# A decoder layer with expert retrieval: seven gather buffers in place of eight, and normalised rows kept in SBUF

## The chip, the cores and the metric

One core of a Trainium2 chip. The time is that of the device, in microseconds (us), for one execution of the whole layer; several executions give a median. Engines: TensorE (PE; PEld is its weight load), VectorE (DVE), ScalarE (ACT), GpSimd (POOL) and SP, which issues DMAs only.

## The reference, cut to what matters

One layer for a prompt of 1024 tokens and a sample group of 8 x 8 tokens, all in float32:

```python
xn = rms_norm(x, attn_norm); proj = xn @ w_in
mixed = concat(differential_attention(proj), rwkv7_time_mixing(proj))
h = x + mixed @ w_out
hn = rms_norm(h, ffn_norm)                 # the "normalised rows"
# PEER retrieval, for each row of hn:
q = hn @ wq                                # 8 heads x 2 x 128
s = q . sub_keys                           # 128 scores per head and half
eidx, gate = top 16 of the 16 x 16 best pairs, softmax
u, v = u_tab[eidx], v_tab[eidx]            # 1024 floats each
y = sum over 8 heads x 16 experts of gate * gelu(u . hn) * v
out = rms_norm(h + y, final_norm)
```

Each row gathers 128 experts, and each expert is one row of 2048 floats (u beside v), 8 KB.

## The kernel before, in words

The rows are cut into nine tiles: t = 0 to 7 of 128 prompt rows each, and t = 8 (`LAST`) of 64 sample rows. One program on every engine holds five stages as Python generators, and each engine issues its part of every stage in the same interleaved order: `run` (L312) first plays `FILL` (L202), which holds the whole input projection and the stages of tiles 0 and 1 ahead of the gathers, then goes through the gather slots, n = 0 to 1087. A tile has 128 slots (64 for the last), and `slots[n]` is (t, j, h): j numbers groups of eight rows, h the head. After each slot the generators of later tiles are pulled by a plan (`pulls`, L261): during the window of tile t (its 128 slots) the time mixing, attention and output stage of tile t + 2 run, and the top-k choice of tile t + 1.

What a slot does, for 8 rows x 16 experts = 128 experts:

- GpSimd gathers 128 expert rows into `buf[n % NBUF]` (L994), 1.05 MB, one row of 8 KB per partition. It waits until the slot that used the buffer before, n - NBUF, has been summed (`v_used`, L993). `NBUF` is 8 (L134).
- VectorE multiplies the u half with `hnR` and sums it into `dot` (L2262). `hnR` holds the group's eight normalised rows, each repeated on 16 partitions.
- ScalarE takes the gelu (L1684) and makes the gate matrix `Z` (L1690), two slots later (`ACT_LAG`).
- TensorE sums gate times v into `psO` (L1413, `v_sum`), three slots later (`SUM_LAG`).

Once per group of eight slots TensorE builds `hnR` for the next group: `repeat_hn` (L1388) multiplies the selection `pick` (made by ScalarE, L1658) with the tile's normalised rows `hn`, into `psH`, in two halves at slots h = 2 and 5. ScalarE copies them to `hnR` (L1666).

The normalised rows come from the output stage, `project_out`. ScalarE squares `op_h` (L1627, into `op_hn` as a throw-away output, with the sum kept) and takes the root; VectorE scales `op_h` into `op_hn` (L2127); TensorE transposes it for the query scores (L1351). SP stores `op_hn` to `scratch_hn_rows` in HBM (L834). At slot 118 of each window (L891) SP's `load_hn` (L852) waits for that store and for the tile's last repeat, and loads the rows of tile t + 1 into `hn`, one place of [128, 1024]. Tile 0's rows are loaded during the fill (L838). A repeat waits for `hn_in` (L1392).

SP issues all other transfers in its own program order: stores of the projection, loads of weights (`op_w`, two of 2 MB, and `op_wkr`, four of 2 MB, per tile), the rows of `h`, y and so on. At step 25 of the output stage it waits, before loading the next tile's time-mixing rows (`load_p`), for `hn_turned`, for the store of `h` and for that of `op_hn` (L842 to L844).

SBUF is laid out by hand; `ip_*` tensors of the projection lie over `buf`, `hnR`, `hn` and `y`, which the gathers use later. So GpSimd starts the gathers only when all the projection's stores have landed (`ip_stored`, L988).

Of the kernel before, what the change touches and what calls it, by code (L numbers as in the profile page):

```python
# [21 lines left out]
ALU = mybir.AluOpType  # L22
# [3 lines left out]
P = 128  # L26
D = 1024
# [81 lines left out]
def rows(t, n=P):  # L109
    return bass.ds(t * P, n)  # L110
# [20 lines left out]


LAST = NT - 1
NBUF = 8  # L134
NZ = 4
QW = 2 * NK
NJ = P // 8
# [145 lines left out]
def peer(nc, T):  # L283
# [100 lines left out]
    with ExitStack() as ctx:  # L384
# [75 lines left out]
            ip_r = e.sb("r", [P, 3, NT])  # L460
        buf = [m.sb(f"buf{b}", [P, 2 * D]) for b in range(NBUF)]
        hnR = m.sb("hnR", [P, 2, D])
        hn = m.sb("hn", [P, D])
        y = m.sb("y", [P, 4, QUART])

        mix = m.sb("mix", [P, D])
# [158 lines left out]
            hn_stored hn_turned hnT scores_done sc_copied""")  # L625
        wk_in = [m.sem(f"op_wk_in{i}") for i in range(2)]
        block = ctx.enter_context(nc.Block())

        def quarters(ap, t):

# [12 lines left out]
        def _(sp):  # L643
# [164 lines left out]
            def project_out(t):  # L808
                R = rows_of(t)

                def load_wk(c_):
                    if t == 0 and c_ == 0:
                        fold_stored()
                    sp.dma_start(wkr[:, c_ % 2].rearrange("p c k n -> p c (k n)"), wk_rows[c_]
                                 ).then_inc(wk_in[c_ % 2], 16)

                for k in range(OP_STEPS):
                    if k == 0:
                        sp.wait_ge(at["o_ready"], t + 1)
                        if t == LAST:  # L820
                            load_w_out(0)
                            load_w_out(1)
                        sp.dma_start(op_h[0:R], T["x"][rows(t, R), :]).then_inc(op["h_in"], 16)
                        sp.dma_start(op_gf[:], T["ffn_norm"].partition_broadcast(P)).then_inc(op["gf_in"], 16)
                    if k == 14:
                        sp.wait_ge(op["summed"], 2 * t + 2)
                        load_wk(0)
                        load_wk(1)
                    if k == 15:
                        sp.wait_ge(op["added"], t + 1)  # L830
                        sp.dma_start(T["h"][rows(t, R), :], op_h[0:R]).then_inc(op["h_stored"], 16)
                    if k == 17:
                        sp.wait_ge(op["hn_ready"], t + 1)
                        sp.dma_start(hn_rows[rows(t, R), :], op_hn[0:R]).then_inc(op["hn_stored"], 16)  # L834
                    if k in (21, 24):
                        sp.wait_ge(op["scores_done"], NC * t + (k - 18) // 3)
                        load_wk((k - 21) // 3 + 2)
                    if k == 25 and t == 1:  # L838
                        sp.wait_ge(ip["summed"], NT)
                        load_hn(0)  # L840
                    if k == 25 and t < LAST:
                        sp.wait_ge(op["hn_turned"], 2 * t + 2)  # L842
                        sp.wait_ge(op["h_stored"], 16 * (t + 1))
                        sp.wait_ge(op["hn_stored"], 16 * (t + 1))  # L844
                        load_p(t + 1)
                    yield

# [2 lines left out]
                    yield  # L850

            def load_hn(t):  # L852
                R = rows_of(t)
                sp.wait_ge(op["hn_stored"], 16 * (t + 1))
                if t:
                    sp.wait_ge(f["hnR_done"], 2 * NJ * t)
                sp.dma_start(hn[0:R, :], hn_rows[rows(t, R), :]).then_inc(f["hn_in"], 16)

            def load_gy(t):

# [18 lines left out]
            def slot(n):  # L879
                t, k = n // PER, n % PER  # L880
                if n == 0:
                    project_stored(NU)
                    load_y(0)
                if t and k == 4:
                    load_gy(t)
                if t and k == 20:
                    store_y(t - 1)
                if t and k == 32:
                    sp.wait_ge(f["y_stored"], 64 * t)
                    load_y(t)  # L890
                if t < LAST and k == 118:  # L891
                    load_hn(t + 1)

            run(slot, {"ip": project, "tm": mix_in_time, "at": attend, "op": project_out, "topk": topk})
            store_y(LAST)
# [104 lines left out]
        def _(pe):  # L1000
# [326 lines left out]
            def project_out(t):  # L1327
                R = rows_of(t)
                for k in range(OP_STEPS):
# [18 lines left out]
                    if k == 17:  # L1348
                        pe.wait_ge(op["hn_ready"], t + 1)
                        for n in range(KD):  # L1350
                            last = nc.tensor.transpose(B[:, n // 4, n % 4 * P:n % 4 * P + R], op_hn[0:R, n * P:(n + 1) * P],  # L1351
                                                       ident[0:R, 0:R])
                            if n % 4 == 3:
                                last.then_inc(op["hn_turned"], 1)
# [33 lines left out]
            def repeat_hn(g_, half):  # L1388

                t, j, _ = slots[g_ * PH]  # L1390
                if half == 0:
                    pe.wait_ge(f["hn_in"], 16 * (t + 1))  # L1392
                    pe.wait_ge(f["pick_ready"], g_ + 1)
                pe.wait_ge(f["hnR_ready"], 2 * g_ + half)
                nc.tensor.matmul(psH[:], pick[:].rearrange("p i k -> p (i k)"),  # L1395
                                 hn[:, half * 512:(half + 1) * 512], start=True, stop=True).then_inc(f["hnR_done"], 1)

            def sum_y(t):

# [36 lines left out]
        def _(act):  # L1436
# [179 lines left out]
            def project_out(t):  # L1616
                R = rows_of(t)
                for k in range(OP_STEPS):
# [5 lines left out]
                                                 ACT.Copy).then_inc(op["copied"], 1)  # L1624
                    if k == 15:
                        act.wait_ge(op["added"], t + 1)
                        nc.scalar.activation(op_hn[0:R], op_h[0:R], ACT.Square, accum_out=st[0:R, 16:17]  # L1627
                                             ).then_inc(op["squared"], 1)
                        act.wait_ge(op["squared"], t + 1)
                        nc.scalar.activation(st[0:R, 17:18], st[0:R, 16:17], ACT.Sqrt, bias=eps[0:R, 0:1],  # L1630
                                             scale=1.0 / D).then_inc(op["root"], 1)
# [61 lines left out]
            def slot(n):  # L1693
                t, j, h = slots[n]
                if n == 0:
                    act.wait_ge(const_in, 16 * CONSTS_IN)
                    make_pick(0)
                    repeat_hn(0, 0)
                    repeat_hn(0, 1)
                if n - h + PH < TOTAL:  # L1700
                    if h == 0:
                        make_pick(n // PH + 1)
                    if h in (4, 7):
                        repeat_hn(n // PH + 1, (h - 4) // 3)
                if n >= ACT_LAG:
                    gate(n - ACT_LAG)
                if t and n == begin(t) + 5:
                    norm_y(t - 1)
                if t and n == begin(t) + 11:
                    root_y(t - 1)  # L1710
# [9 lines left out]
        def _(dve):  # L1720
# [394 lines left out]
            def project_out(t):  # L2115
                R = rows_of(t)
                for k in range(OP_STEPS):
# [5 lines left out]
                    if k == 16:  # L2123
                        dve.wait_ge(op["root"], t + 1)
                        dve.wait_ge(op["gf_in"], 16 * (t + 1))
                        chain(nc.vector.reciprocal(st[0:R, 18:19], st[0:R, 17:18]))
                        nc.vector.scalar_tensor_tensor(op_hn[0:R], op_h[0:R], st[0:R, 18:19], op_gf[0:R], ALU.mult,  # L2127
                                                       ALU.mult).then_inc(op["hn_ready"], 1)
                    yield

# [251 lines left out]
```

## Time and profile before

| | us |
|---|---|
| median of 3 runs | 3982.27 |
| lowest, highest | 3975.95, 3983.49 |
| the profiled execution | 3977.58 |
| its span in the profile | 3975.8 |

The profile is of one execution. Its page gives for each engine the busy time (part 1), the course over 40 equal slices (part 2, with the clock granted to TensorE and the rate of the DMA engines), the DMA queues (part 3), the chain of work that ended last, followed back from the end (part 4), and the costliest groups of instructions with the idle time before them and what ended it (part 5). Beside the page the trace was asked for the timeline of single engines, for windows and for single lines. Gathers run from 747.7 us to 3944.7 us.

### The profile page before, as it was taken

The numbers are of one execution on the slowest core, as the hardware profiler recorded it, in microseconds if no ns is written. First come the engines' busy times: TensorE is split into PE (matmuls) and PEld (weight loads), VectorE is DVE, ScalarE is ACT, GpSimd is POOL, SyncE is SP. The second block draws the span as 40 slices with busy tenths as digits, with TensorE's granted clock in tenths as the row PEclk, the third lists the DMA queues.
The fourth block names the chain that finished last, engine by engine and source line by source line (L and its number), as shares of the span: only waits on it lengthen the run. The fifth ranks groups of instructions, "written<-read, shape, count | busy, mean of one in ns | idle before, by whom it ended". The sixth has DMA issues, their size and how long they took to land.

```text
span 3975.8 us, 54677 instructions
## 1 busy us (share of the span) xinstructions
PE 2853.9 (72%) x20366; PEld 1358.9 (34%) x20366; DVE 2600.8 (65%) x5836; ACT 1284.4 (32%) x3597; POOL 1358.7 (34%) x1190
## 2 busy tenths in 40 slices
PE   6899999675667576766766766677566758867564
PEld 3654454342224232322332243224222415521111
DVE  2423455488668848884987598658866776445954
ACT  1311211324333424342434334433433234422222
POOL 1000000243344434443434343434333456534443
PEclk9999999877877787788778777788787666777655
DMA  9535414899999999999999999999999999999998
GB/s 311 196 141 182 175 67 165 330 400 397 420 416 394 409 421 407 416 402 419 411 404 387 417 409 409 388 417 406 387 409 392 352 375 411 381 399 420 407 405 350
DMA packets 254682, 1431.66 MB, mean 360 GB/s; under 512 B 27376, under 2 KB 45312, under 8 KB 110160
## 3 DMA queue, kind: packets, MB, share of 16 engines
q0 software_dynamic: 163232, 1162.26, 72.1%
q1 hardware_dynamic: 91184, 265.89, 17.7%
q8 instruction: 161, 2.64, 0.3%
q14 instruction: 105, 0.86, 0.1%
HBM read 1373.21 MB, written 54.85 MB: 359 GB/s over the span
## 4 chain that ended last, share of the span: by engine, by line
PE 38%; DMA 32%; DVE 21%; issue 4%; ACT 2%; POOL 2%; SPq 0%; DVEq 0%; ACTq 0%; POOLq 0%
DMA pe_buf<-in_experts,pe_idx 28%; PE ip_B L1027 9%; DVE pe_buf L2262 7%; PE pe_psO L1413 5%; PE pe_B L1361 4%; PE pe_psH L1395 3%; PE pe_B L1344 3%; DMA op_wkr<-scratch_wk_rows 2%; PE pe_B L1061 1%; PE pe_B L1212 1%; DMA ip_w<-in_w_in 1%; POOL pe_buf L994 1%; DVE pe_top L2032 1%; DMA op_w<-in_w_out 1%; PE pe_B L1253 1%
## 5 line engine op out<-in xcount | busy, mean ns | idle before, releaser
L994 POOL DMA_INDIRECT pe_buf<-in_experts,pe_idx x1088 | 1277.3, 1174 | 2500.6 <-PE pe_psO L1413 1702.5
L2262 DVE CUSTOM_DVE_ANT_0 pe_buf<-pe_buf,pe_hnR 128x1024 f32<-128x1024 f32 x1088 | 1319.2, 1224 | 781.6 <-DMA pe_buf<-in_experts,pe_idx 768.5
L1413 PE MATMUL pe_psO<-pe_buf,pe_Z 128*32 128x256 f32 x8704 | 830.1, 485 | 547.2 <-ACT pe_Z L1690 510.4
L1413 PEld LDWEIGHTS pe_psO<-pe_buf,pe_Z 128*32 128x32 f32 x8704 | 222.9, 124 | 1187.3 <-ACT pe_Z L1690 888.3
L1684 ACT ACTIVATE pe_gelu<-pe_dot 128x1 f32<-128x1 f32 x1088 | 217.3, 200 | 1273.1 <-DVE pe_dot L2262 1270.3
L1395 PE MATMUL pe_psH<-pe_hn,pe_pick 128*128 128x512 f32 x544 | 402.9, 831 | 63.9 <-ACT pe_hnR L1666 61.6
L1027 PE MATMUL ip_B<-ip_w,ip_xT 128*128 128x512 f32 (+1 forms) x1008 | 433.3, 580 | 16.6 <-DMA ip_w<-in_w_in 16.6
L1690 ACT ACTIVATE pe_Z<-pe_gl,pe_gelu 128x8 f32<-128x8 f32 x1088 | 327.2, 301 | 43.0 <-ACT pe_gelu L1684 0.4
L1361 PE MATMUL pe_B<-op_wkr,pe_mix 128*128 128x512 f32 (+1 forms) x576 | 264.9, 604 | 9.2 <-DMA op_wkr<-scratch_wk_rows 9.2
L1027 PEld LDWEIGHTS ip_B<-ip_w,ip_xT 128*128 128x128 f32 x1008 | 190.8, 195 | 213.5 <-issue 208.1
L1666 ACT ACTIVATE pe_hnR<-pe_psH 128x512 f32<-128x512 f32 x272 | 159.0, 584 | 49.5 <-PE pe_psH L1395 48.8
L1395 PEld LDWEIGHTS pe_psH<-pe_hn,pe_pick 128*128 128x128 f32 x544 | 107.5, 243 | 193.7 <-ACT pe_hnR L1666 95.9
L1344 PE MATMUL pe_B<-op_w,op_mT 128*128 128x512 f32 (+1 forms) x288 | 153.2, 661 | 11.9 <-DMA op_w<-in_w_out 11.9
L1361 PEld LDWEIGHTS pe_B<-op_wkr,pe_mix 128*128 128x128 f32 (+1 forms) x576 | 101.8, 185 | 144.4 <-issue 143.9
L1781 DVE TENSOR_TENSOR ip_o<-ip_o,ip_mu 128x512 f32<-128x512 f32 (+1 forms) x36 | 22.5, 625 | 163.4 <-ACT ip_o L1454 159.2
L1246 PE MATMUL pe_B<-pe_ident,at_prob 128*128 128x128 f32 x144 | 37.3, 419 | 115.5 <-DVE at_prob L2040 115.5
L1212 PE MATMUL pe_B<-tm_Tn,tm_ML 64*64 64x64 f32 x1312 | 61.8, 256 | 73.8 <-DVE tm_Tt L1912 51.0
L1684 ACT ACT_TABLE_LOAD x79 | 101.4, 1283 | 1.4
L2262 DVE DVE_READ_ACCUMULATOR2_ANT pe_dot<- 128x1 f32 x1088 | 89.3, 82 | 0.0
L1454 ACT ACTIVATE ip_o<-ip_B,ip_r 128x512 f32<-128x512 f32 (+1 forms) x45 | 29.0, 644 | 186.4 <-PE ip_B L1027 183.5
L1212 PEld LDWEIGHTS pe_B<-tm_Tn,tm_ML 64*64 64x64 f32 x1312 | 55.2, 167 | 98.1 <-DVE tm_Tt L1912 59.7
L1142 PE MATMUL pe_B<-tm_Tt,tm_X 64*64 64x64 f32 x1312 | 87.4, 240 | 0.0
(344 smaller groups left out, 3616.5 us busy)
## 6 DMA issues: line engine op xcount, KB each, us to landing
op_wkr<-scratch_wk_rows SPq DMA_DIRECT2D x36, 2048.0 KB, 11.8
ip_w<-in_w_in SPq DMA_DIRECT2D x18, 2048.0 KB, 9.1
op_w<-in_w_out SPq DMA_DIRECT2D x18, 2048.0 KB, 19.8
pe_buf<-in_experts,pe_idx POOLq DMA_INDIRECT x1088, 13.8
ip_w<-in_peer_wq SPq DMA_DIRECT2D x4, 2048.0 KB, 11.1
scratch_wk_rows<-wk_wkc SPq DMA_DIRECT2D x16, 512.0 KB, 6.2
tm_p<-scratch_kept_rows SPq DMA_DIRECT2D x8, 896.0 KB
tm_ps<-scratch_moved_rows SPq DMA_DIRECT2D x8, 896.0 KB
```

Of the source, the lines that this page charges most:

```text
L994: pool.indirect_dma_start(buf[b][:], None, T["experts"], bass.IndirectOffsetOnAxis(ap=idx[:, t % 2, h * NJ + j:h * NJ + j + 1], axis=0)).t ...
L1027: last = nc.tensor.matmul(ipB[:, bank_of(g), 0:cols_of(n)], ip_xT[:, t % MOST, k, :], ip_w[:, load % 2, k, 0:cols_of(n)], start=(k == 0), ...
L1142: last = nc.tensor.matmul(B[cp, bank, 256 + col:256 + col + CH], X[cp, h, :], Tt[cp, h, :], start=True, stop=True)
L1212: last = nc.tensor.matmul(B[cp, h // 4, h % 4 * CH:(h % 4 + 1) * CH], ML[cp, lv % 2, h, :], rhs, start=True, stop=True)
L1344: last = nc.tensor.matmul(B[0:R, 2 + half, :], op_mT[:, n, 0:R], w_out[:, n, half * 512:(half + 1) * 512], start=(n == 0), stop=(n == KD - 1))
L1361: last = nc.tensor.matmul(B[0:R, n_, :], mix[:].rearrange("p (k t) -> p k t", k=KD)[:, n, 0:R], wkr[:, n_ % 2, :, n, :], start=(n == 0), s ...
L1395: nc.tensor.matmul(psH[:], pick[:].rearrange("p i k -> p (i k)"), hn[:, half * 512:(half + 1) * 512], start=True, stop=True).then_inc(f["h ...
L1413: last = nc.tensor.matmul(psO[32 * x:32 * x + 32, j // 4, :], Z[:, n % NZ, 24 - 8 * turn:56 - 8 * turn], buf[n % NBUF][:, D + x * QUART:D ...
L1666: nc.scalar.activation(hnR[:, g_ % 2, half * 512:(half + 1) * 512], psH[:], ACT.Copy).then_inc(f["hnR_ready"], 1)
L1684: nc.scalar.activation(gelu[:, col:col + 1], dot[:, col:col + 1], ACT.Gelu_apprx_tanh).then_inc(f["gelu_done"], 1)
L1690: nc.scalar.activation(Z[:, n % NZ, 24:32], gl[:, n // PH % 2, h, :], ACT.Copy, scale=gelu[:, col:col + 1]).then_inc(f["Z_ready"], 1)
L2262: nc.vector.tensor_tensor_reduce(buf[b][:, 0:D], buf[b][:, 0:D], hnR[:, n // PH % 2, :], 1.0, 0.0, ALU.mult, ALU.add, dot[:, n % (NBUF):n ...
```

## The change

`NBUF` goes from 8 to 7, and `hn` from one place of 4 KB per partition to three, which together take the same room: 8 x 8 + 4 = 7 x 8 + 12 = 68 KB. Tile t's rows live in place (t + 2) % 3 (`hn_of`). For t of 2 and above the output stage writes them there at once: `op_hn_of(t)` is then that place, and ScalarE, VectorE and TensorE use it in the stead of `op_hn`. The store, the load and the waits on them are gone for those tiles; TensorE's repeats wait for `hn_ready` of the output stage. Before ScalarE writes to a place that a tile has used (t of 3 and above) it waits until the repeats of tile t - 3 are done. Tiles 0 and 1 (`BOUNCED`) keep their way over HBM, since during the fill their places still hold the projection's tensors; tile 1's load moves from slot 118 of window 0 to its slot 1. As the buffers have moved, `hnR` now lies over the projection's output buffers, and ScalarE waits for the projection's stores before its first `pick`.

```diff
@@ constants
-NBUF = 8
+NBUF = 7
+BOUNCED = 2
@@ SBUF
-        hn = m.sb("hn", [P, D])
+        hn = m.sb("hn", [P, 3, D])
+        def hn_of(t):
+            return hn[:, (t + 2) % 3]
+        def op_hn_of(t):
+            return op_hn if t < BOUNCED else hn_of(t)
@@ SP: project_out
                     if k == 17:
-                        sp.wait_ge(op["hn_ready"], t + 1)
-                        sp.dma_start(hn_rows[rows(t, R), :], op_hn[0:R]).then_inc(op["hn_stored"], 16)
+                        if t < BOUNCED:
+                            sp.wait_ge(op["hn_ready"], t + 1)
+                            sp.dma_start(hn_rows[rows(t, R), :], op_hn[0:R]).then_inc(op["hn_stored"], 16)
...
-                        sp.wait_ge(op["hn_stored"], 16 * (t + 1))
+                        sp.wait_ge(op["hn_stored"], 16 * min(t + 1, BOUNCED))
                         load_p(t + 1)
@@ SP: load_hn, slot
                 sp.wait_ge(op["hn_stored"], 16 * (t + 1))
-                if t:
-                    sp.wait_ge(f["hnR_done"], 2 * NJ * t)
-                sp.dma_start(hn[0:R, :], hn_rows[rows(t, R), :]).then_inc(f["hn_in"], 16)
+                sp.dma_start(hn_of(t), hn_rows[rows(t), :]).then_inc(f["hn_in"], 16)
...
-                if t < LAST and k == 118:
-                    load_hn(t + 1)
+                if n == 1:
+                    load_hn(1)
@@ TensorE: project_out, repeat_hn
-    ... nc.tensor.transpose(..., op_hn[0:R, n * P:(n + 1) * P], ident[0:R, 0:R])
+    ... nc.tensor.transpose(..., op_hn_of(t)[0:R, n * P:(n + 1) * P], ident[0:R, 0:R])
...
-                    pe.wait_ge(f["hn_in"], 16 * (t + 1))
+                    if t < BOUNCED:
+                        pe.wait_ge(f["hn_in"], 16 * (t + 1))
+                    else:
+                        pe.wait_ge(op["hn_ready"], t + 1)
...
-                                 hn[:, half * 512:(half + 1) * 512], ...
+                                 hn_of(t)[:, half * 512:(half + 1) * 512], ...
@@ ScalarE: project_out, slot
                         act.wait_ge(op["added"], t + 1)
-                        nc.scalar.activation(op_hn[0:R], op_h[0:R], ACT.Square, ...
+                        if t >= 3:
+                            act.wait_ge(f["hnR_done"], 2 * NJ * (t - 2))
+                        nc.scalar.activation(op_hn_of(t)[0:R], op_h[0:R], ACT.Square, ...
...
                 if n == 0:
                     act.wait_ge(const_in, 16 * CONSTS_IN)
+                    for i in range(2):
+                        act.wait_ge(ip_stored[i], stored_of(NU, i))
                     make_pick(0)
@@ VectorE: project_out
-                        nc.vector.scalar_tensor_tensor(op_hn[0:R], op_h[0:R], ...
+                        nc.vector.scalar_tensor_tensor(op_hn_of(t)[0:R], op_h[0:R], ...
```

How the instructions move. On SP, the output stage of tile 2 in window 0, before the change (`op_wkr` are the score weights, `scratch_h` the rows of h, `tm_p` and `tm_ps` the next tile's time-mixing rows):

```order
L814 DMA op_wkr<-scratch_wk_rows 128x4096 [waits pe_op_summed]
L814 DMA op_wkr<-scratch_wk_rows 128x4096
L831 DMA scratch_h<-op_h 128x1024 [waits pe_op_added]
L834 DMA scratch_hn_rows<-op_hn 128x1024 [waits pe_op_hn_ready]
L814 DMA op_wkr<-scratch_wk_rows 128x4096 [waits pe_op_scores_done]
L857 DMA pe_hn<-scratch_hn_rows 128x1024 [waits pe_fg_hnR_done,pe_op_hn_stored]
L814 DMA op_wkr<-scratch_wk_rows 128x4096 [waits pe_op_scores_done]
L739 DMA tm_p<-scratch_kept_rows 128x1792 [waits pe_ip_stored0,pe_op_hn_stored,pe_ip_stored1,pe_op_h_stored,pe_op_hn_turned]
L740 DMA tm_ps<-scratch_moved_rows 128x1792
```

The same place now:

```order
L822 DMA op_wkr<-scratch_wk_rows 128x4096 [waits pe_op_summed]
L822 DMA op_wkr<-scratch_wk_rows 128x4096
L839 DMA scratch_h<-op_h 128x1024 [waits pe_op_added]
L822 DMA op_wkr<-scratch_wk_rows 128x4096 [waits pe_op_scores_done] x2
L747 DMA tm_p<-scratch_kept_rows 128x1792 [waits pe_ip_stored0,pe_op_hn_stored,pe_ip_stored1,pe_op_h_stored,pe_op_hn_turned]
L748 DMA tm_ps<-scratch_moved_rows 128x1792
```

The store of the rows and, between two weight loads, the load of the next tile's rows are gone, with the waits for `hn_ready`, `hnR_done` and `hn_stored` that stood on them; the one `hn_stored` that `tm_p` keeps asks for tile 1's store only.

On ScalarE, slot 0, where the gathers begin, before the change (`pe_pick` selects the rows, `pe_hnR` holds the repeated ones):

```order
L1454 ACTIVATE ip_o<-ip_B,ip_r 128x256 [waits pe_ip_scaled,pe_ip_stored0,pe_ip_done]
L1658 ACTIVATE pe_pick<-pe_ident 128x128 [waits pe_fg_hnR_done,pe_const_in]
L1666 ACTIVATE pe_hnR<-pe_psH 128x512 [waits pe_fg_hnR_done] x2
L1658 ACTIVATE pe_pick<-pe_ident 128x128 [waits pe_fg_hnR_done]
L1684 ACT_TABLE_LOAD
L1684 ACTIVATE pe_gelu<-pe_dot 128x1 [waits pe_fg_dotted]
```

and now:

```order
L1463 ACTIVATE ip_o<-ip_B,ip_r 128x256 [waits pe_ip_scaled,pe_ip_stored0,pe_ip_done]
L1669 ACTIVATE pe_pick<-pe_ident 128x128 [waits pe_ip_stored1,pe_fg_hnR_done,pe_ip_stored0,pe_const_in]
L1677 ACTIVATE pe_hnR<-pe_psH 128x512 [waits pe_fg_hnR_done] x2
L1669 ACTIVATE pe_pick<-pe_ident 128x128 [waits pe_fg_hnR_done]
L1695 ACT_TABLE_LOAD
L1695 ACTIVATE pe_gelu<-pe_dot 128x1 [waits pe_fg_dotted]
```

The order is the same; the first `pe_pick` waits in addition for the two semaphores of the projection's stores, as GpSimd's first gather does.

## Rows read from the trace of the kernel before

**Rows 1.** The page, part 1: busy time, share of the span, instructions.

```profile
PE 2853.9 (72%) x20366; PEld 1358.9 (34%) x20366; DVE 2600.8 (65%) x5836; ACT 1284.4 (32%) x3597; POOL 1358.7 (34%) x1190
```

**Rows 2.** The page, part 2: DMA share in tenths and GB/s in 40 slices.

```profile
DMA  9535414899999999999999999999999999999998
GB/s 311 196 141 182 175 67 165 330 400 397 420 416 394 409 421 407 416 402 419 411 404 387 417 409 409 388 417 406 387 409 392 352 375 411 381 399 420 407 405 350
```

**Rows 3.** The page, part 4: chain that ended last, shares of the span.

```profile
PE 38%; DMA 32%; DVE 21%; issue 4%; ACT 2%; POOL 2%; SPq 0%; DVEq 0%; ACTq 0%; POOLq 0%
DMA pe_buf<-in_experts,pe_idx 28%; PE ip_B L1027 9%; DVE pe_buf L2262 7%; PE pe_psO L1413 5%; PE pe_B L1361 4%; PE pe_psH L1395 3%; PE pe_B L1344 3%; DMA op_wkr<-scratch_wk_rows 2%; PE pe_B L1061 1%; PE pe_B L1212 1%; DMA ip_w<-in_w_in 1%; POOL pe_buf L994 1%; DVE pe_top L2032 1%; DMA op_w<-in_w_out 1%; PE pe_B L1253 1%
```

**Rows 4.** Windows of 25 us in tile 5; columns: busy, PEclk, DMA share, GB/s.

```profile
2836.00:2861.00 25.00, 11.12 (x76) 5.96 (x76) 21.60 (x42) 14.03 (x29) 5.79 (x6) 0.70 1.00 404
2861.00:2886.00 25.00, 17.38 (x115) 9.82 (x116) 22.17 (x54) 10.84 (x25) 9.25 (x7) 0.75 0.76 291
2886.00:2911.00 25.00, 15.41 (x117) 5.44 (x115) 19.88 (x50) 11.59 (x34) 14.87 (x12) 0.86 0.98 390
2911.00:2936.00 25.00, 22.09 (x123) 7.53 (x122) 18.35 (x35) 8.51 (x27) 11.05 (x11) 1.00 1.01 420
2936.00:2961.00 25.00, 8.25 (x47) 3.67 (x47) 10.20 (x18) 9.74 (x22) 4.12 (x5) 0.66 1.01 424
```

**Rows 5.** The page, part 5: the gathers, with GpSimd's idle time.

```profile
L994 POOL DMA_INDIRECT pe_buf<-in_experts,pe_idx x1088 | 1277.3, 1174 | 2500.6 <-PE pe_psO L1413 1702.5
```

**Rows 6.** Timeline of GpSimd: start, us, instruction, idle before and releaser.

```profile
888.59 0.94 POOL L994 DMA_INDIRECT pe_buf<-in_experts,pe_idx  x1 [7.38 <-PE pe_psO L1413]
...
2847.24 1.57 POOL L994 DMA_INDIRECT pe_buf<-in_experts,pe_idx  x1 [10.77 <-PE pe_psO L1413]
...
2958.68 0.94 POOL L994 DMA_INDIRECT pe_buf<-in_experts,pe_idx  x1 [13.38 <-PE pe_psO L1413]
...
3550.26 0.94 POOL L994 DMA_INDIRECT pe_buf<-in_experts,pe_idx  x1 [10.97 <-PE pe_psO L1413]
```

**Rows 7.** Chain of waits from 2830 to 2900 us: start, us, what.

```profile
2835.91 1.24 DVE pe_top L2032
...
2842.77 1.97 PE pe_B L1246 x8
```

**Rows 8.** Line L994 in tile 5, then in the whole run: gathers and landing.

```profile
L994 POOL DMA_INDIRECT pe_buf<-in_experts,pe_idx x127: 932/941/2676, 2634.3 to 3013.8; - x127
...
DMA to landing us min/median/max: 7.5/14.1/26.9
...
DMA to landing us min/median/max: 5.8/13.8/28.8
```

**Rows 9.** DMA issues of the normalised rows: count, KB, us to landing.

```profile
scratch_hn_rows<-op_hn SPq DMA_DIRECT2D x8, 512.0 KB, 7.8
pe_hn<-scratch_hn_rows SPq DMA_DIRECT2D x8, 512.0 KB, 8.5
```

**Rows 10.** Line L1395: what ended TensorE's idle time before it.

```profile
  ACT pe_hnR L1666: 157.5, 76
```

**Rows 11.** Timeline of SP at the end of window 0.

```profile
1068.13 0.32 SPq L834 DMA_DIRECT2D scratch_hn_rows<-op_hn  x1
...
1091.00 0.32 SPq L857 DMA_DIRECT2D pe_hn<-scratch_hn_rows  x1
1095.15 0.32 SPq L814 DMA_DIRECT2D op_wkr<-scratch_wk_rows  x1
```

**Rows 12.** Timeline of the first gathers.

```profile
744.01 0.31 ACT L1658 ACTIVATE pe_pick<-pe_ident 128x128 f32<-128x128 f32 x1
...
745.55 0.60 ACT L1666 ACTIVATE pe_hnR<-pe_psH 128x512 f32<-128x512 f32 x1 [1.23 <-PE pe_psH L1395]
...
747.68 1.03 POOL L994 DMA_INDIRECT pe_buf<-in_experts,pe_idx  x1 [663.96 <-DMA scratch_kept_rows<-ip_o]
...
755.32 1.22 DVE L2262 CUSTOM_DVE_ANT_0 pe_buf<-pe_buf,pe_hnR 128x1024 f32<-128x1024 f32 x1 [10.14 <-DMA pe_buf<-in_experts,pe_idx]
```

More of the change, by code:

```diff
@@ L852, in load_hn @@
             def load_hn(t):
-                R = rows_of(t)
                 sp.wait_ge(op["hn_stored"], 16 * (t + 1))
-                if t:
-                    sp.wait_ge(f["hnR_done"], 2 * NJ * t)
-                sp.dma_start(hn[0:R, :], hn_rows[rows(t, R), :]).then_inc(f["hn_in"], 16)
+                sp.dma_start(hn_of(t), hn_rows[rows(t), :]).then_inc(f["hn_in"], 16)
             def load_gy(t):
@@ L1350, in project_out @@
                         for n in range(KD):
-                            last = nc.tensor.transpose(B[:, n // 4, n % 4 * P:n % 4 * P + R], op_hn[0:R, n * P:(n + 1) * P],
+                            last = nc.tensor.transpose(B[:, n // 4, n % 4 * P:n % 4 * P + R], op_hn_of(t)[0:R, n * P:(n + 1) * P],
                                                        ident[0:R, 0:R])
@@ L1395, in repeat_hn @@
                 nc.tensor.matmul(psH[:], pick[:].rearrange("p i k -> p (i k)"),
-                                 hn[:, half * 512:(half + 1) * 512], start=True, stop=True).then_inc(f["hnR_done"], 1)
+                                 hn_of(t)[:, half * 512:(half + 1) * 512], start=True, stop=True).then_inc(f["hnR_done"], 1)
             def sum_y(t):
@@ L1626, in project_out @@
                         act.wait_ge(op["added"], t + 1)
-                        nc.scalar.activation(op_hn[0:R], op_h[0:R], ACT.Square, accum_out=st[0:R, 16:17]
+                        if t >= 3:
+                            act.wait_ge(f["hnR_done"], 2 * NJ * (t - 2))
+                        nc.scalar.activation(op_hn_of(t)[0:R], op_h[0:R], ACT.Square, accum_out=st[0:R, 16:17]
                                              ).then_inc(op["squared"], 1)
@@ L2126, in project_out @@
                         chain(nc.vector.reciprocal(st[0:R, 18:19], st[0:R, 17:18]))
-                        nc.vector.scalar_tensor_tensor(op_hn[0:R], op_h[0:R], st[0:R, 18:19], op_gf[0:R], ALU.mult,
+                        nc.vector.scalar_tensor_tensor(op_hn_of(t)[0:R], op_h[0:R], st[0:R, 18:19], op_gf[0:R], ALU.mult,
                                                        ALU.mult).then_inc(op["hn_ready"], 1)
```

## The prediction

> **What bounds the kernel now.** Start with the page. No compute engine is full over the span: TensorE leads with 72% [rows 1]. The second part shows why: from slice 9 of 40 on, when the expert gathers begin, nearly every slice has the 16 DMA engines at nine tenths or more, moving about 400 to 420 GB/s [rows 2]. The chain that ended last agrees, but only partly: 32% of it is DMA, 38% TensorE and 21% VectorE [rows 3]. So two regimes must be told apart: stretches in which transfers set the pace, and stretches in which computing does and the DMA engines starve.
>
> The windows of 25 us show both. A saturated slice has a DMA share of 1.01 and 420 GB/s; a starved one has 0.76 and 291 GB/s [rows 4]. In tile 5 the slices from 2836 to 2911 lose speed while those beside them do not. What starves them is the buffer loop: GpSimd spends 1702.5 us idle waiting for v_sum (L1413) to free a buffer [rows 5]. Its timeline has 38 waits of at least 7 us, from 888.6 to 3550.3 us; 15 of them are over 9.9 us [rows 6]; shown are the first, the last and two of tile 5. At the starved place the chain runs through attention (VectorE's maxima at L2032, then TensorE's products), not through a gather [rows 7].
>
> How full is the loop? In tile 5 127 gathers are issued in 379.5 us, one per 3.0 us, with a median of 14.1 us to landing [rows 8]. 14.1 / 3.0 = 4.7 gathers are in flight; the other 3.3 buffers are landed, being used or being freed. One gather is 128 rows of 8 KB, 1.05 MB, or 2.5 us of DMA time at 416 GB/s. A gather lands after 5.8 us at the earliest [rows 8], 2.5 of it data, so about 3.3 us pass in which a new gather moves nothing. The DMA engines run dry when the time between two issues exceeds 14.1 - 3.3 = 10.8 us, which is a wait of 9.9 us plus 0.94 of issuing. (An estimate from medians: single places scatter around it.)
>
> **The change, part by part.**
> *Removed transfers.* Stores and loads of normalised rows go for tiles 2 to 8: six of 0.524 MB and a last of 0.262 MB, both ways, 6.8 MB. Each took 7.8 and 8.5 us to land [rows 9], but nothing waits for that long: of TensorE's idle time before L1395 most is ended by ScalarE and none by a DMA [rows 10]. They cost bandwidth alone. They are issued in the last part of a tile [rows 11], where the slices run at 420 to 424 GB/s [rows 4], so their time is real: 6.8 MB / 416 GB/s = **-16 us**.
>
> *One buffer less.* Held buffers stay 3.3, since holding is set by the lag of gate and v_sum; those in flight fall from 4.7 to 3.7. Where transfers set the pace this costs nothing: a shorter queue just lands sooner, about 11 us instead of 14. The cost is at the long waits. The dry point moves from a wait of 9.9 us to 9.9 - 3.0 = 6.9 us. (a) The 15 waits above 9.9 go dry one gather sooner: 15 x 2.5 = 38 us. (b) The other 23, mostly 7 to 9 us, go dry for about 0.9 us each: 21 us. (c) Six of the 15, one in each of tiles 0 to 5, come like the one that ends at 2958.7 [rows 6]: SP has just queued wk loads of 2 MB, and the slice keeps 424 GB/s [rows 4]. Take back 6 x 2.5 = 15. The sum is 38 + 21 - 15 = **+44 us**. Bounds: 0, if computing absorbs every one of them [rows 7], and 38 x 2.5 = 95 us, if each costs a whole gather. I take 44, since the starved slices of rows 4 show that waits of this kind already cost DMA time with eight buffers: the slices at 2836, 2861 and 2886 together miss (16 + 129 + 30) / 420 x 25 = 10 us.
>
> A page's rule bears on this. In the trace the fastest gather needs 5.8 us, 3.3 more than its data. The Trainium skill, "DMA: Bandwidth & Descriptors", section "Anatomy of one DMA — SWDGE (gpsimd) path", puts a transfer issued by GpSimd at about 2.0 us fixed plus its bytes over 436 GB/s. By it a gather takes 4.4 us, and the dry points lie at waits of 11.2 and 8.2 us instead of 9.9 and 6.9; (a), (b) and (c) would give about 22, 18 and 15, that is 25 us instead of 44 and a time of 3987 us. The trace's 5.8 us speaks against so short a fixed part, unless the other gathers in the queue lengthen it.
>
> *Waits on SP.* SP no longer waits for hn_ready (L833) or for later hn_stored (L844). Behind them it waits for scores_done (L836) and for hn_turned and the store of h (L842, L843), which are the later ones. At slot 118 it drops the wait for hnR_done; the wk load behind it waits for scores anyway, 4 us later [rows 11]. 0 us; without that cover the loads of the next tile would come a little sooner, a gain.
>
> *New wait on ScalarE at slot 0.* Before, ScalarE makes pick at 744.0; now not until the last store of the projection has landed, which is what releases GpSimd at 747.7. From there pick (0.3), a repeat (1.2 with its wait), copy (0.6), and both once more end near 752; the first dot starts at 755.3, when its gather lands [rows 12]. Hidden with 3 us to spare. Queued behind it on ScalarE are the gelu of slot 0, which waits for that dot, and TensorE's repeats. 0 us; without the cover 3.5.
>
> *Other edits.* ScalarE's wait for hnR_done at L1626 is met a whole tile ahead (the output stage of tile t runs during tile t-2, the place was last read during t-3). TensorE waits for hn_ready instead of hn_in: older too. Tile 1's load moves from slot 118 to slot 1, where SP queues 0.5 MB behind eight gathers: same bytes. 0 us each.
>
> Sum: -16 + 44 = **+28 us**. The profiled execution took 3977.6 us (span 3975.8), 4.7 under the median of the three runs, so I forecast 3977.6 + 28, rounded to **4005 us**, 0.7% over the profiled time. A measurement of this kernel can tell about 0.2%, 8 us, from no change.
>
> **The rivals.**
> *A. Absorbed: faster.* At the starved place the chain goes through attention. If a gather lands one place later and its dot was going to wait for VectorE anyway, only the removed traffic shows: 3977.6 - 16 = 3961 us. For it: [rows 7]. Against it: after such a stretch transfers set the pace again, and DMA time lost is not made up. It decides from the point where the lost buffer costs under 8 us in all, that is, under 0.2 us at each of the 38 waits.
> *B. Half absorbed: no measurable change.* Two waits that belong to one attention stretch cost one gather, not two; then about half of the 44 us, 15 to 25, is lost and the time is 3977 to 3987. The 3987 us worked out above with the fixed cost of the Trainium skill's page on DMA lies at its upper edge; the chance of that rule is counted here.
> *C. Every long wait costs a full gather: slower.* 3977.6 + 95 - 16 = 4057 us, 79 over the profiled time. For it: median landings hide that many gathers wait behind SP's 2 MB loads. Against: most waits are only just over 7 us.
> *D. The bytes leave, but at no gain.* If the removed transfers ran in starved moments, -16 becomes 0 and the forecast 4021. The 420 GB/s beside them speak against it.
>
> **How the numbers follow.** The forecast with D, 3990 to 4030, gets 0.46; A 0.21; B 0.21; C and anything above 4030, 0.12. Slower by over 0.2%: 0.46 + 0.12 = 0.58; within 0.2%: 0.21; faster: 0.21. The range runs from A's value, 3961, which is also the bound of nothing lost, to 4042, between D and C; about 0.1 lies below it (scatter around A) and 0.08 above. The likeliest case alone: 3990 to 4030.
>
> **What the profile after would show.** Right: gathers land after about 11 us instead of 13.8; slices at the attention places fall below 291 GB/s or widen; saturated slices stay at 416 to 420; waits on GpSimd for v_sum grow, and no store or load of hn is left but those of tiles 0 and 1. Tiles come out about 3 us longer each: 44 us over eight tiles, less 2 for the traffic. Wrong: if tiles shorten by 2 us each, A holds; if saturated slices too fall under 410 GB/s, in-flight depth matters everywhere, and the loss exceeds C. A first dot later than 755.3 would make the new wait on ScalarE the culprit.

## The result, and the profile after

| | us |
|---|---|
| the changed kernel, median of 5 runs | 4036.5 (4031.8 to 4047.5) |
| the kernel before, in the same comparison | 3982.3 (3975.7 to 3999.1) |
| ratio, with its 95% interval | 1.0136 (1.0116 to 1.0156) |
| the profiled execution, and its span | 4047.5, 4045.7 |

The change makes the kernel slower by 1.36%, 54 us. The way was forecast, the size was not: I had +28 us. The profiled execution is the slowest of the five, and the one of before lay under its median, so the two spans are 70 us apart and not 54.

The page of the changed kernel, the rate in 40 slices (part 2) and two groups of part 5 (busy, mean ns of one, idle before, releaser):

```profile
GB/s 297 201 144 188 157 89 177 335 383 406 421 401 406 387 411 403 371 387 418 406 393 391 414 385 377 409 408 388 362 419 365 332 372 371 351 392 420 396 402 354
...
L1000 POOL DMA_INDIRECT pe_buf<-in_experts,pe_idx x1088 | 1278.1, 1175 | 2563.5 <-PE pe_psO L1422 1749.0
L2275 DVE CUSTOM_DVE_ANT_0 pe_buf<-pe_buf,pe_hnR 128x1024 f32<-128x1024 f32 x1088 | 1321.5, 1224 | 842.6 <-DMA pe_buf<-in_experts,pe_idx 825.6
```

The gather phase keeps its peak of 420 GB/s in some slices, but others sink: 371 and 332 are there, where before had 352 as its lowest between the first gathers and the tail [rows 2]. Single slices prove little: the page of e5 below, faster than before, has one of 344. So I laid windows of 25 us end to end over the eight prompt tiles, from the first gather on. The DMA share is under 0.95 in 11 of 121 windows before and in 24 of 124 now. That count scatters too: it is 14 in e2 below, a kernel with eight buffers that is a little faster than before. GpSimd waits 1749.0 us for v_sum, 47 more than before [rows 5]. VectorE, which multiplies each gathered row, now waits 825.6 us for gathers. Before it was 768.5:

```profile
L2262 DVE CUSTOM_DVE_ANT_0 pe_buf<-pe_buf,pe_hnR 128x1024 f32<-128x1024 f32 x1088 | 1319.2, 1224 | 781.6 <-DMA pe_buf<-in_experts,pe_idx 768.5
```

These 57 us are most of the 70 between the two executions. VectorE's own work is the same (1319.2 and 1321.5 us busy), its data comes later. The wait by itself does not measure a kernel: it is 805.4 us in e6 below, which is faster than before, and 615.7 us in e11, which is slower.

The normalised rows' transfers are down to those of tiles 0 and 1 (the view of DMA issues: count, KB, us to landing), where [rows 9] had eight full ones (and the last tile's half one, which those rows don't show):

```profile
scratch_hn_rows<-op_hn SPq DMA_DIRECT2D x2, 512.0 KB, 15.3
pe_hn<-scratch_hn_rows SPq DMA_DIRECT2D x2, 512.0 KB, 9.8
```

At the attention place of tile 5, windows of 25 us (busy by engine, then PEclk, DMA share, GB/s), against [rows 4]; the place comes 36 us later here:

```profile
2872.00:2897.00 25.00, 10.88 (x76) 5.96 (x76) 21.88 (x42) 14.02 (x29) 7.87 (x7) 0.78 0.90 354
2897.00:2922.00 25.00, 16.66 (x110) 9.26 (x111) 22.23 (x59) 10.84 (x25) 8.72 (x7) 0.74 0.78 300
2922.00:2947.00 25.00, 14.34 (x116) 5.25 (x115) 16.52 (x39) 10.78 (x32) 13.13 (x12) 0.74 0.94 376
```

Against 420 GB/s the three slices miss (66 + 120 + 44) / 420 x 25 = 13.7 us, before 10.4. The place that I took for the typical one costs 3.3 us more. A larger loss stands in tile 2, where before shows hardly any. Windows there, before:

```profile
1622.00:1647.00 25.00, 23.62 (x241) 13.70 (x240) 22.34 (x50) 7.73 (x25) 10.09 (x10) 0.89 1.01 412
1647.00:1672.00 25.00, 14.78 (x152) 6.59 (x150) 22.77 (x58) 9.67 (x26) 11.84 (x11) 0.79 1.01 420
1672.00:1697.00 25.00, 16.14 (x102) 7.28 (x105) 20.17 (x49) 10.92 (x30) 8.42 (x8) 0.66 1.01 415
```

and in the changed kernel, shifted by the 9 us that it is late there:

```profile
1631.00:1656.00 25.00, 24.48 (x170) 14.50 (x169) 16.33 (x38) 4.33 (x16) 6.64 (x6) 0.50 0.82 320
1656.00:1681.00 25.00, 18.31 (x186) 9.54 (x184) 19.82 (x46) 9.20 (x25) 11.20 (x10) 0.77 0.82 329
1681.00:1706.00 25.00, 16.60 (x84) 5.63 (x84) 19.44 (x47) 6.94 (x21) 8.83 (x7) 0.59 1.02 417
```

Before, the slices miss 13 / 420 x 25 = 0.8 us, now (100 + 91 + 3) / 420 x 25 = 11.5 us. GpSimd's timeline there, before (start, us, instruction, idle before and its releaser):

```profile
1611.83 0.94 POOL L994 DMA_INDIRECT pe_buf<-in_experts,pe_idx  x1 [5.34 <-PE pe_psO L1413]
...
1626.45 1.65 POOL L994 DMA_INDIRECT pe_buf<-in_experts,pe_idx  x1 [7.39 <-PE pe_psO L1413]
...
1636.31 0.94 POOL L994 DMA_INDIRECT pe_buf<-in_experts,pe_idx  x1 [3.28 <-PE pe_psO L1413]
...
1642.73 1.17 POOL L994 DMA_INDIRECT pe_buf<-in_experts,pe_idx  x1 [4.24 <-PE pe_psO L1413]
```

and now:

```profile
1635.89 1.40 POOL L1000 DMA_INDIRECT pe_buf<-in_experts,pe_idx  x1 [7.66 <-PE pe_psO L1422]
...
1652.09 0.94 POOL L1000 DMA_INDIRECT pe_buf<-in_experts,pe_idx  x1 [7.53 <-PE pe_psO L1422]
...
1661.27 1.93 POOL L1000 DMA_INDIRECT pe_buf<-in_experts,pe_idx  x1 [7.01 <-PE pe_psO L1422]
```

Before it is a series of middling waits, 5.3, 7.4, 3.3 and 4.2 us within 31 us, and the DMA engines stay full through it (share 1.01). With seven buffers the same series has 7.7, 7.5 and 7.0 us within 26 us, and the share falls to 0.82 in two slices.

The buffer is not the only difference at this place. TensorE's granted clock is 0.50 in the window at 1631, its lower level all through, where before has 0.89 at the same place, and TensorE, full of time-mixing products there, is busy 24.48 of the 25 us. The v sums that free the buffers stand in line behind these products. For comparison the 25 us that begin 146 us after tile 2's first gather, with eight buffers (before, then e2) and with seven (e1, then the changed kernel):

```profile
1632.37:1657.37 25.00, 20.09 (x253) 12.26 (x251) 21.07 (x46) 6.81 (x22) 11.33 (x11) 1.00 1.01 416
1625.45:1650.45 25.00, 19.54 (x194) 10.61 (x186) 19.88 (x43) 6.12 (x20) 11.38 (x10) 0.83 0.93 361
1656.71:1681.71 25.00, 20.48 (x213) 11.23 (x209) 19.45 (x44) 5.31 (x18) 10.31 (x10) 0.85 0.87 335
1647.68:1672.68 25.00, 24.18 (x240) 14.13 (x238) 16.73 (x39) 5.26 (x17) 8.48 (x8) 0.74 0.64 243
```

At nearly the same clock (0.83 and 0.85) seven buffers give 335 GB/s and eight 361; with a clock of 1.00 eight give 416, with 0.74 seven give 243. So I take from tile 2 that places beside the attention run dry, not what each costs, nor that the buffer alone makes it.

### The profile page after: what moved, and what is told of

Same layout as the page of the kernel before. It is cut to its first block, busy times and chain, and to the rows that moved or that the text cites. A ratio compares the mean times of both kernels' runs of the same rounds, so it can differ in the third digit from the quotient of the medians.

```text
span 4045.7 us, 54662 instructions
## 1 busy us (share of the span) xinstructions
PE 2877.1 (71%) x20366; PEld 1361.6 (34%) x20366; DVE 2604.2 (64%) x5836; ACT 1284.1 (32%) x3597; POOL 1364.7 (34%) x1190
## 4 chain that ended last, share of the span: by engine, by line
DMA 31%; PE 24%; DVE 17%; issue 5%; ACT 2%; POOL 2%; another core or an unknown queue 0%; DVEq 0%; SPq 0%; ACTq 0%; POOLq 0%
DMA pe_buf<-in_experts,pe_idx 28%; DVE pe_buf L2275 6%; PE pe_psO L1422 6%; PE pe_B L1367 4%; PE pe_psH L1404 3%; DMA op_wkr<-scratch_wk_rows 2%; POOL pe_buf L1000 1%; PE pe_B L1350 1%; PE pe_B L1320 1%; PE pe_B L1067 1%; PE pe_B L1218 1%; DMA op_w<-in_w_out 1%; DVE pe_top L2045 1%; PE pe_B L1246 1%; ACT L1695 1%
## 5 line engine op out<-in xcount | busy, mean ns | idle before, releaser
L1000 POOL DMA_INDIRECT pe_buf<-in_experts,pe_idx x1088 | 1278.1, 1175 | 2563.5 <-PE pe_psO L1422 1749.0
L2275 DVE CUSTOM_DVE_ANT_0 pe_buf<-pe_buf,pe_hnR 128x1024 f32<-128x1024 f32 x1088 | 1321.5, 1224 | 842.6 <-DMA pe_buf<-in_experts,pe_idx 825.6
L1404 PE MATMUL pe_psH<-pe_hn,pe_pick 128*128 128x512 f32 x544 | 414.5, 854 | 69.1 <-ACT pe_hnR L1677 60.8
L1654 ACT ACTIVATE pe_scores<-pe_B 128x512 f32<-128x512 f32 (+1 forms) x36 | 21.4, 596 | 225.5 <-PE pe_B L1367 225.5
L1067 PE MATMUL pe_B<-pe_Sp,tm_qrT 128*64 128x128 f32 x256 | 65.1, 342 | 34.2 <-DVE pe_Sp L2015 33.5
```

What stands on the lines that cost most here:

```text
L1000: pool.indirect_dma_start(buf[b][:], None, T["experts"], bass.IndirectOffsetOnAxis(ap=idx[:, t % 2, h * NJ + j:h * NJ + j + 1], axis=0)).t ...
L1067: nc.tensor.matmul(B[cp, bank, pr * P:(pr + 1) * P], qrT[:, n, pr, cp], Sp[:, pr].rearrange("p k i -> p (k i)"), start=True, stop=False, s ...
L2275: nc.vector.tensor_tensor_reduce(buf[b][:, 0:D], buf[b][:, 0:D], hnR[:, n // PH % 2, :], 1.0, 0.0, ALU.mult, ALU.add, dot[:, n % (NBUF):n ...
```

## The experiments

The ratios are to the kernel before, timed beside it on the same chip, with 95% intervals. Medians of the kernel before differ by up to 13 us between such comparisons, so ratios are what is compared.

### Is it the buffer, or the rows kept in SBUF?

Seven buffers and nothing else:

```diff
-NBUF = 8
+NBUF = 7
...
         buf = [m.sb(f"buf{b}", [P, 2 * D]) for b in range(NBUF)]
+        m.sb("hold_buf", [P, 2 * D])
         hnR = m.sb("hnR", [P, 2, D])
```

> The kernel before with seven buffers and nothing else changed (the eighth's room stays empty, the rows still go over HBM). Theory 1, the lost buffer makes the whole loss and the removed transfers give back 16 us: 4037 + 16 = 4053 us, +70 on before. Theory 2, the loss comes from the kept rows (the new wait on ScalarE, the places in SBUF, the writes by the output stage) and depth costs little: 3982 to 3995 us. My prediction's own term for depth, +44, would give 4026.

Measured: 4038.8 us, ratio 1.0165 (1.0142 to 1.0189), so +66 us on 3982. Its page shows low slices like those of the changed kernel (364 and 348 GB/s):

```profile
GB/s 306 192 142 189 158 87 178 334 382 408 421 404 364 393 421 402 393 394 419 405 372 381 417 397 383 399 416 377 375 405 375 348 350 399 394 394 420 399 399 353
```

The DMA share is under 0.95 in 21 of 124 windows. Theory 1 stands; the loss is there without any of the kept rows. The other half, eight buffers without the transfers of tiles 2 to 8:

```diff
-                    if k == 17:
+                    if k == 17 and t < 2:
                         sp.wait_ge(op["hn_ready"], t + 1)
...
-                        sp.wait_ge(op["hn_stored"], 16 * (t + 1))
+                        sp.wait_ge(op["hn_stored"], 16 * min(t + 1, 2))
...
-                if t < LAST and k == 118:
+                if t < 1 and k == 118:
...
-                    pe.wait_ge(f["hn_in"], 16 * (t + 1))
+                    pe.wait_ge(f["hn_in"], 16 * min(t + 1, 2))
```

> The kernel before, eight buffers, with the stores and loads of the normalised rows of tiles 2 to 8 and the waits on them left out; the gathers of those tiles use tile 1's rows, so that part of the computation is changed. Theory 1: 6.8 MB less at 416 GB/s, 16 us: 3966 us. Rival, the transfers ran in starved moments: 3978 to 3982 us.

Measured: 3957.7 us, ratio 0.9962 (0.9944 to 0.9980), -15 us. The rival falls, since the interval leaves out 1. With +66 the two halves make +51, and the whole change has +54. Nothing of a size that these runs can tell (each of the three is known to 7 to 9 us) is left for the new waits or the places in SBUF.

### How the cost grows with each buffer

The changed kernel with six buffers (`NBUF = 6`, with a `hold_buf` of one buffer as above):

> The changed kernel with six buffers. Theory 1a, each buffer less in flight costs more than the last, since more waits outlast the queue: 54 + 16 = 70 us for the first, over 100 for the second, so 4140 to 4160 us. Theory 1b, only the few longest waits count and each costs one gather more: +40 to +50, 4080 us. Theory 2: 4037 us.

Measured: 4187.3 us, ratio 1.0547 (1.0521 to 1.0573). The second buffer costs 1.0547 - 1.0136 = 4.1%, about 164 us, well above my 1a and more than twice the first. 1b falls.

But is it depth itself, or depth beside the other stages? The last tile answers from the traces at hand: during its 64 slots no stage of a later tile runs. A window of 100 us inside it, of the kernel before:

```profile
3820.00:3920.00 100.00, 58.92 (x330) 12.26 (x330) 50.19 (x86) 27.79 (x94) 47.77 (x39) 0.52 1.02 416
```

of the changed kernel:

```profile
3890.00:3990.00 100.00, 57.20 (x331) 12.12 (x330) 50.27 (x86) 27.78 (x94) 51.08 (x39) 0.57 1.01 416
```

and with six buffers:

```profile
4020.00:4120.00 100.00, 56.01 (x332) 12.38 (x332) 50.47 (x88) 28.04 (x96) 54.08 (x40) 0.60 1.02 416
```

416 GB/s and a full DMA share (1.01 or 1.02) each time. Six buffers are enough to keep the DMA engines full when no other stage delays the freeing of a buffer. So the eighth and the seventh are there for the delays that the other stages make. In the eight tiles before it, 40 of 129 windows of the kernel with six buffers have a share under 0.95.

### Does attention make it?

Attention of prompt tiles cut to two blocks of keys, on the three engines that work on it, with eight buffers and with seven:

```diff
-                    n = (t + 1) * P
+                    n = min(t + 1, 2) * P
...
-                                for b in range(t + 1):
+                                for b in range(min(t + 1, 2)):
...
-    vs[:, b, h * VD:(h + 1) * VD], start=(b == 0), stop=(b == t))
+    vs[:, b, h * VD:(h + 1) * VD], start=(b == 0), stop=(b == min(t, 1)))
```

> The kernel before with attention of prompt tiles cut to two blocks of keys at most (part of the attention is left out), so its VectorE, ScalarE and TensorE steps stay as short as in tile 1. Both theories: faster than before by at most the time the DMA engines starve at the attention places, 10 to 50 us: 3920 to 3960 us. It is the partner of e7.

> The same with seven buffers. Theory 1c, the loss of a buffer is made at the long waits of attention: e7 minus e6 at most 20 us, in place of 65. Theory 1d, it is made wherever in-flight gathers run low, all over the tile: e7 minus e6 50 us or more.

Measured: 3948.2 us, ratio 0.9935 (0.9910 to 0.9960), and 3995.9 us, ratio 1.0067 (1.0040 to 1.0094). The buffer still costs 1.32%, 48 us between the medians, against 1.65% with the whole attention. The intervals leave open how much the large attention adds, if anything; most of the cost comes without it. That is 1d, at the edge of what I had written for it (50 us or more): the cost is not that of a few long attention waits. Windows with a share under 0.95 are 5 of 120 with eight buffers and 10 of 122 with seven.

The pair also answers whether a lower TensorE clock makes the loss, since the mean granted clock was 0.785 in the profiled execution of the changed kernel and 0.790 before. In the profiled executions of e6 and e7 it is 0.780 in both, and their spans are 3958.4 and 4002.4 us: 44 us apart at one clock.

Their gathers, e6 and then e7, are used below:

```profile
L994 POOL DMA_INDIRECT pe_buf<-in_experts,pe_idx x1088: 932/940/4127, 747.1 to 3927.2; - x182
...
DMA to landing us min/median/max: 5.4/14.3/29.9
...
L995 POOL DMA_INDIRECT pe_buf<-in_experts,pe_idx x1088: 935/942/4127, 745.7 to 3973.9; - x182
...
DMA to landing us min/median/max: 5.6/12.3/25.5
```

### Holding each buffer for less time

A buffer is held from its landing to the v sum. `ACT_LAG` and `SUM_LAG` put the gate two slots and the v sum three slots behind the dot. In the changed kernel:

```diff
-ACT_LAG, SUM_LAG = 2, 3
+ACT_LAG, SUM_LAG = 1, 2
```

> The changed kernel with the gate one slot after the dot (was two) and the sum of v two slots after it (was three). Theory 1: a buffer is held for less time where lag sets it; of the 3 us of a slot perhaps half is regained, half the lost buffer: 35 us, 4000 us. Rival, holding is set by the other stages' work on TensorE and ScalarE, or the shorter lag makes TensorE wait for Z: 4037 us or above.

Measured: 3965.0 us, ratio 0.9986 (0.9972 to 0.9999). Against the changed kernel's 1.0136 that is -1.5%, 60 us: not half of the lost buffer but nearly all of it. The rival falls. The line of the gathers, and its time to landing:

```profile
L1000 POOL DMA_INDIRECT pe_buf<-in_experts,pe_idx x1088: 932/946/4128, 738.5 to 3930.2; - x182
...
DMA to landing us min/median/max: 5.5/13.3/27.6
```

(3930.2 - 738.5) / 1087 = 2.94 us per gather and 13.3 us to landing are 4.5 in flight, out of seven: 2.5 are held. In the kernel before, 13.8 us [rows 8] at 2.94 us were 4.7 out of eight, with 3.3 held. With six buffers and the long lag:

```profile
L1001 POOL DMA_INDIRECT pe_buf<-in_experts,pe_idx x1088: 932/941/4129, 748.4 to 4147.0; - x182
...
DMA to landing us min/median/max: 5.4/10.1/22.2
```

10.1 / 3.13 = 3.2 in flight. The times go with the number in flight, not with the number of buffers: 4.5 with seven is within 0.2% of 4.7 with eight (e4 also moves 6.8 MB less, worth 0.4% in e2), and 3.2 costs 5.5%. With attention cut short it is the same: 14.3 / 2.93 = 4.9 of eight in flight and 12.3 / 2.97 = 4.1 of seven, for the 1.32%.

The same edit with eight buffers:

> The kernel before (eight buffers, rows over HBM) with the gate one slot and the v sum two slots behind the dot. Depth theory: the shorter holding acts like two thirds of a buffer more, but with eight the next buffer is worth less than the 65 us of the eighth; about -35 us on before, ratio 0.991. Rival, the shorter lag itself speeds the engines up whatever the depth: as with seven buffers, -60 us or more, ratio 0.985.

Measured: 3960.5 us, ratio 0.9973 (0.9959 to 0.9987), -11 us. A gain, but a third of what I expected; the rival, 60 us or more whatever the depth, falls. With this lag 5.2 gathers are in flight:

```profile
L994 POOL DMA_INDIRECT pe_buf<-in_experts,pe_idx x1088: 935/942/4132, 745.0 to 3921.3; - x182
...
DMA to landing us min/median/max: 5.9/15.2/28.9
```

so the step from 4.7 to 5.2 is worth 0.3%. GpSimd's waits of over 9.9 us for v_sum fall from 15 to 2, and these 11 us are all that comes of it. Of the kernels here that do the whole layer this one is the fastest, with e4 (0.9986) close behind.

The fourth corner of the square, seven buffers and the short lag with the rows over HBM:

> Seven buffers, rows over HBM as before, gate one slot and v sum two slots behind the dot. It completes a square with before, e1 and e5. Theory 3, the cost of the lost buffer depends on how long a buffer is held: with the long lag it is 65 us, here e4 and the 15 us of the removed transfers say 3980 us, 20 us over e5. Rival, depth costs 65 us whatever the lag, and e4's gain had another cause: 4025 us.

Measured: 3986.3 us, ratio 1.0006 (0.9986 to 1.0026). And six buffers in the changed kernel:

> The changed kernel with six buffers and the short lag. Theory 3: the short lag gives back more the fewer the buffers (10 us with eight, 60 with seven), so well over 60 us of e3's 4187: about 4070 us. Rival, the gain saturates at 60 us: 4125 us.

Measured: 4036.5 us, ratio 1.0149 (1.0125 to 1.0172). In ratios:

| | lag 2, 3 | lag 1, 2 |
|---|---|---|
| 8 buffers, rows over HBM | 1.0000 | 0.9973 |
| 7 buffers, rows over HBM | 1.0165 | 1.0006 |
| 7 buffers, rows kept | 1.0136 | 0.9986 |
| 6 buffers, rows kept | 1.0547 | 1.0149 |

The lost buffer costs 1.65% with the long lag and 0.33% with the short one, 66 and 13 us. That is theory 3, below its 20 us but inside the intervals. With the short lag and seven buffers 14 windows of 25 us have a share under 0.95, in e9 (of 122) as in e4 (of 121), against 21 and 24 with the long one. For six buffers the short lag gives 4%, near 160 us and more than the 117 I had. The value of a buffer is not a constant of the kernel; it depends on how long the others are held.

### How short can the lag be?

With eight buffers, first the gate in the dot's own slot and the v sum one behind (`0, 1`), then both one slot behind (`1, 1`):

> The kernel before with the gate in the dot's own slot and the v sum one slot behind. Depth theory: holding shrinks again, a little under e5 (another -5 to -15 us). Rival, ScalarE and TensorE now stall on the dot in their own order and delay the other stages: slower than e5, up to before's time or above.

Measured: 4034.4 us, ratio 1.0153 (1.0122 to 1.0183). The rival holds. Its gathers land after 13.9 us, one is issued every 2.99 us, so 4.6 are in flight, nearly as many as before, and it is 1.5% slower: the number in flight tells the time only as long as the consumers themselves are not held up.

> Eight buffers, the gate one slot and the v sum also one slot behind the dot. If e8's loss came from the gate in the dot's own slot, this stays at e5's time, 3960 us or a few below; if TensorE waiting for Z in its own slot makes it, it is as slow as e8, 4030 us.

Measured: 4020.3 us, ratio 1.0096 (1.0064 to 1.0127). Part 5 of its page, the dot and the v sum:

```profile
L2262 DVE CUSTOM_DVE_ANT_0 pe_buf<-pe_buf,pe_hnR 128x1024 f32<-128x1024 f32 x1088 | 1311.6, 1222 | 627.8 <-DMA pe_buf<-in_experts,pe_idx 615.7
...
L1413 PE MATMUL pe_psO<-pe_buf,pe_Z 128*32 128x256 f32 x8704 | 883.2, 496 | 949.4 <-ACT pe_Z L1690 927.6
```

and the v sum with lag 1, 2 and eight buffers:

```profile
L1413 PE MATMUL pe_psO<-pe_buf,pe_Z 128*32 128x256 f32 x8704 | 845.0, 486 | 637.9 <-ACT pe_Z L1690 632.4
```

VectorE waits less for gathers than in any kernel above but e8 (615.7 us; e8 593.7), but TensorE now stands 927.6 us before the v sum until ScalarE has made Z, in e8 848.3, against 632.4. While it stands there, the other stages' products behind it in its order cannot start. I had expected e11 to be as fast as e5 or as slow as e8; it is slow, if a little less so. Both `0, 1` and `1, 1` put the v sum one slot behind the dot and differ in where the gate stands. So one slot from dot to v sum is too near, wherever the gate is, and costs more than it frees. Whether the gate may stand in the dot's own slot with the v sum two behind (`0, 2`) was not tried.

## Why the prediction was right or wrong

**Removed transfers: right.** -16 us forecast; -15 by e2, and 0.29% between e1 and the changed kernel, 12 us, though from two comparisons. Rival D is out. (Its 4021 and my 4005 are 4021.6 and 4005.6 by their sums.)

**One buffer less: right in kind, too small.** The term was +44 us and measured +66. The step that failed is "the dry point moves from a wait of 9.9 us to 9.9 - 3.0 = 6.9 us", and the count of 38 waits above it. It takes each wait alone, lets it begin with the median 3.7 gathers in flight, and prices nothing below 6.9 us, where the trace of before has 48 more waits for v_sum of 5 to 7 us. What the runs show in its place: +66 us, with windows under a share of 0.95 up from 11 to 21 (e1), and most of the loss there without the long attention waits (48 us with attention cut short). At the attention place of tile 5, where (a) had two whole gathers, 5 us, the slices lost 3.3. In tile 2 the waits come in a series, none over 7.4 us before, and places there went dry that the count priced at next to nothing; the lower clock has its part in that. That a series keeps the queue from filling up again is how I read this place; no run takes such a series apart, so why these places run dry stays open in part. Had the sum come out right, it would have done so for a wrong reason. Nor do the long waits tell the loss: e8 has none over 9.9 us and is 1.5% slower than before. Part (c), the 15 us taken back for waits beside wk loads, was not tried by itself.

**Lower ends.** "Absorbed" and "half absorbed", rivals A and B, are out. So is the 25 us that I derived from the Trainium skill, "DMA: Bandwidth & Descriptors", section "Anatomy of one DMA — SWDGE (gpsimd) path": by its 2.0 us fixed part depth should matter even less than I thought, and 66 us were measured. The trace does not agree with a gather of 4.4 us either: in no trace that tells landings did one take under 5.4 us. Whether other transfers in the queue make the difference was not tried; what failed in both sums is the count of waits. At the upper end, rival C's 95 us for the buffer is more than the 66 measured.

**Held buffers "stay 3.3".** Not quite. With six buffers and the same lag 10.1 us at 3.13 leave 2.8 held; with attention cut short it is 3.1 of eight and 2.9 of seven, so the lost buffer took 0.75 gathers from those in flight and not a whole one. A part of holding may be waiting for VectorE, which shrinks as data comes later; that was not measured. I had named the lag as what sets holding, and drew nothing from it; e4 and e5 show that this was the better lever.

**New wait on ScalarE: right.** The timeline of the first gathers, against [rows 12]:

```profile
749.56 0.31 ACT L1669 ACTIVATE pe_pick<-pe_ident 128x128 f32<-128x128 f32 x1 [3.22 <-issue]
...
749.76 1.02 POOL L1000 DMA_INDIRECT pe_buf<-in_experts,pe_idx  x1 [662.65 <-DMA scratch_kept_rows<-ip_o]
...
754.81 0.60 ACT L1677 ACTIVATE pe_hnR<-pe_psH 128x512 f32<-128x512 f32 x1 [2.16 <-PE pe_psH L1404]
...
757.57 1.23 DVE L2275 CUSTOM_DVE_ANT_0 pe_buf<-pe_buf,pe_hnR 128x1024 f32<-128x1024 f32 x1 [10.18 <-DMA pe_buf<-in_experts,pe_idx]
```

`pick` now starts at 749.56, with GpSimd's first gather at 749.76, and the second copy ends at 755.4; the dot waits for its gather until 757.57. 2.2 us to spare. That all is 2 us later than before comes from the projection's last stores, issued 2.2 us later in this execution.

**Waits on SP and the rest.** Nothing is left over between e1 plus e2 (+51 us) and the change (+54 us), within intervals of 7 to 9 us each.

**What I said the profile would show.** Waits for v_sum grew (47 us), as said. The attention slices did not fall below 291 GB/s; they widened (354, 300, 376). The landing time of the changed kernel is not told by its trace; the nearest are 12.3 us with seven buffers in e7, where I had 11, and 10.1 with six. The prompt tiles came out 8.4 us longer on average from first gather to first gather (1.8 to 14.8), not 3. And windows that were full before (412 and 420 GB/s in tile 2) fell far under 410, which I had called a sign that depth matters everywhere; the loss did not exceed C for that.

## What to carry to other kernels

Count a prefetch ring by what is in flight: landing time over time per item, with the rest held. A buffer's worth depends on how long consumers hold the others, so look first at whether they can let go sooner: here one slot less of lag was worth nearly a whole buffer of 8 KB per partition with seven buffers and a sixth of one with eight, and a second slot less cost more than it gave. When depth is taken away, don't price only the longest waits: places that are full with the old depth may be the ones to go dry, where middling waits come in a series. Before putting such a place down to the depth, compare the granted clock there.

## What the runs showed that I had not expected

Fewer buffers cost nothing by themselves: in the last tile, with no later tile's stages beside them, gathers of 1.05 MB run at 416 GB/s with eight, seven and six buffers. Beside the other stages the second buffer taken away costs 2.5 times the first (4.1% and 1.65%), while at the other end half a gather more in flight (e5) was worth 0.3%.
